# Four conditioning slots in the second layer's FFN, residual rows restored in two steps, and the first down tile staged one unit sooner

## What is computed

```python
for l in range(DEPTH):
    need_ctx = l < DEPTH - 1
    mod_x = (s_c @ w_mod[l] + b_mod[l])[:, None, :]
    mod_c = s_cc @ w_mod[l] + b_mod[l]
    ...
    h_x = _layer_norm(ALPHA * h_x + ga_x * (mix_x @ w_out[l]), ln_g[l, 0], ln_b[l, 0])
    f_x = _conv_ffn(h_x * (1.0 + cf_x) + sf_x, ffn_w_up[l], ffn_conv_w[l], ffn_conv_b[l], ffn_w_down[l])
    h_x = _layer_norm(ALPHA * h_x + gf_x * f_x, ln_g[l, 1], ln_b[l, 1])

def _conv_ffn(h, w_up, conv_w, conv_b, w_down):
    u = h @ w_up
    up = jnp.pad(u, ((0, 0), (1, 1), (0, 0)))
    u = up[:, :-2] * conv_w[0] + up[:, 1:-1] * conv_w[1] + up[:, 2:] * conv_w[2] + conv_b
    a, v = jnp.split(u, 2, axis=-1)
    return (jax.nn.silu(a) * v) @ w_down
```

## Time and profile before

| | before |
|---|---|
| median of 3 runs | 1996.57 us (1995.75 to 1996.68) |
| profiled execution | 2004.46 us |
| its span | 2002.6 us |
| mean granted TensorE clock | 0.975 |
| PE, DVE, POOL, ACT busy | 95%, 65%, 46%, 45% |
| layer 0 up stage | about 614 to 996 us of the span |
| layer 1 up stage | about 1626 to 1868 us of the span |

### The profile page before, as it was taken

The page is one execution under the profiler, slowest core; times in us unless marked ns, Lnnn a source line. Parts: engine busy times, 40 slices in busy tenths (PEclk is TensorE's granted clock), DMA queues, the critical chain, the costliest instruction groups (busy, mean ns, idle before and its releaser), DMA issues.

```text
span 2002.6 us, 32824 instructions
## 1 busy us (share of the span) xinstructions
PE 1895.2 (95%) x12510; PEld 1606.9 (80%) x12510; DVE 1307.8 (65%) x2566; ACT 898.8 (45%) x1917; POOL 926.5 (46%) x770
## 2 busy tenths in 40 slices
PE   6899799999999999999999999998999989999997
PEld 4788798867778888878888878898877778778786
DVE  3248999676585999999744263999776842222545
ACT  3224588577533222222343342565567543333442
POOL 3145467111345345553353335756432545775643
PEclk9999899999999999999999999999999999999999
DMA  8563000210111333233221121101130212222321
GB/s 349 210 241 114 26 23 22 96 49 2 43 63 43 127 126 118 93 118 117 103 74 63 53 105 64 59 28 43 43 122 1 88 47 98 105 84 91 120 98 71
DMA packets 27372, 177.31 MB, mean 89 GB/s; under 512 B 2896, under 2 KB 4048, under 8 KB 8144
## 3 DMA queue, kind: packets, MB, share of 16 engines
q1 hardware_dynamic: 22976, 158.16, 21.8%
q10 hardware_dynamic: 4240, 17.04, 2.1%
HBM read 171.00 MB, written 4.19 MB: 87 GB/s over the span
## 4 chain that ended last, share of the span: by engine, by line
PE 69%; DVE 13%; POOL 6%; issue 5%; ACT 3%; DMA 2%; SPq 0%; DVEq 0%; ACTq 0%; POOLq 0%
PE PS L1270 20%; PE PS L1165 18%; PE PS L881 9%; PE PS L875 4%; PE PS L1127 3%; PE PS L1105 3%; POOL WS L2412 3%; PE PS L1014 2%; DMA WR<-in_weights 2%; PE PS L1089 2%; DVE W L1687 2%; DVE U L1922 1%; PE PS L1095 1%; PE PS L810 1%; DVE W L2031 1%
## 5 line engine op out<-in xcount | busy, mean ns | idle before, releaser
L1270 PE MATMUL PS<-XH,WS 128*128 128x512 f32 x2016 | 543.6, 356 | 4.6 <-POOL WS L2412 4.6
L1270 PEld LDWEIGHTS PS<-XH,WS 128*128 128x128 f32 x2016 | 360.5, 190 | 60.2 <-issue 4.9
L1270 PE MATMUL PS<-XL,WS 128*128 128x512 f32 x1008 | 358.6, 356 | 0.0
L2412 POOL TENSOR_TENSOR WS<-WR,WS 128x1024 fp32r<-128x1024 f32 x88 | 215.5, 2450 | 289.1 <-ACT WS L1558 288.7
L1623 ACT ACTIVATE W<-PS,PR 128x768 f32<-128x768 f32 (+1 forms) x88 | 78.0, 886 | 424.6 <-PE PS L1270 360.7
L2241 DVE SCALAR_TENSOR_TENSOR W<-PS,PR,W 128x511 f32<-128x511 f32 (+1 forms) x132 | 83.0, 657 | 208.2 <-ACT W L1623 208.2
L1270 PEld LDWEIGHTS PS<-XL,WS 128*128 128x128 f32 x1008 | 191.5, 190 | 26.6
L881 PE MATMUL PS<-EU,XH 128*128 128x256 f32 x624 | 190.1, 305 | 5.6 <-issue 4.6
L2349 POOL TENSOR_TENSOR WL<-WR,EU 128x512 fp32r<-128x512 f32 x96 | 128.8, 1368 | 126.0 <-ACT EU L1327 126.0
L881 PE MATMUL PS<-EU,HL 128*128 128x256 f32 x624 | 182.4, 292 | 0.0
L881 PE MATMUL PS<-WL,XH 128*128 128x256 f32 x624 | 182.3, 292 | 0.0
(11 more groups left out here) (220 smaller groups left out, 4259.1 us busy)
## 6 DMA issues: line engine op xcount, KB each, us to landing
WR<-in_weights SPq DMA_DIRECT2D x128, 1024.0 KB, 4.8
U<-in_weights SPq DMA_DIRECT2D x16, 1024.0 KB, 7.5
U<-in_bias ACTq DMA_DIRECT2D x2, 1792.0 KB, 9.4
H<-in_x SPq DMA_DIRECT2D x1, 2048.0 KB, 7.8
H<-in_x ACTq DMA_DIRECT2D x1, 2048.0 KB, 14.5
U<-in_ln_rows ACTq DMA_DIRECT2D x2, 1024.0 KB, 4.8
WR<-in_weights SPq DMA_DIRECT2D x4, 512.0 KB, 3.5
kept<-H ACTq DMA_DIRECT2D x4, 512.0 KB, 2.6
```

The costliest lines, as they stand in the source:

```text
L1270: mm = pe.matmul(PS[u.pos][:, lo:hi], w[:, part, k, :], src[:, k, lo:hi], start=(k == 0 and src is xh3 and part == 0), stop=(k == KT - 1 a ...
L2412: pool.tensor_tensor(ws5[:, u.c % 2, 1], half_slot(u), ws5[:, u.c % 2, 0], ALU.subtract).then_inc(w_low, 1)
```

## The change

Three edits.

1. Slots 20 to 23 of layer 1 leave layer 0's FFN and go behind units 2, 4, 15 and 17 of layer 1's. They hold the gate of layer 1's FFN, which is read after its up stage. In layer 0 a slot stands behind units 2 to 20 without 6, 10, 14 and 18. The ring places and the counts of the semaphores follow.
2. `restore` becomes `rescale` and `shift_row`: behind the gate products of unit 5 and up, one instruction a unit, so twelve units in layer 0 (5 to 16) and eight in layer 1 (5 to 12).
3. ACT stages the first tile of the down products before the last unit's sum, in place of after it; for that the entries of the down stage are reordered so that the first tile doesn't lie in the up stage's input.

```diff
+LATE = 20
-def mods_behind(j):
+def mods_behind(l, j):
-    return int(1 < j <= 25 - EARLY)
+    if l == 0:
+        return int(1 < j <= 20 and j not in (6, 10, 14, 18))
+    return int(j in (2, 4, 15, 17))
...
-        nxt = list(range(EARLY, 24)) if l + 1 < DEPTH else []
+        nxt = list(range(EARLY, LATE) if l + 1 < DEPTH else range(LATE, 24))
...
-                   [whole(t[:, e * ENTRY:(e + 1) * ENTRY]) for t in (XH, XL, EW) for e in range(2)])
+                   [whole(t[:, e * ENTRY:(e + 1) * ENTRY]) for t, e in ((EW, 0), (XH, 0), (XH, 1), (XL, 0), (XL, 1), (EW, 1))])
...
-                u.kind, u.l, u.j, u.key = "mod", key[1] - 1, key[2], key
+                u.kind, u.l, u.j, u.key = "mod", int(key[2] >= LATE), key[2], key
...
                     if u is real[-1]:
+                        high_tiles(2 * l + 1, k_tiles[2 * l + 1][0])
                         gate(FT - 1)
                     act.wait_ge(up_sum, u.c + 1)
-                    if u is real[-1]:
-                        high_tiles(2 * l + 1, k_tiles[2 * l + 1][0])
...
-            def restore(m, t):
+            def rescale(m, t):
...
                 pool.tensor_tensor(row, row, gain, ALU.mult).then_inc(h_scaled, 1)
+
+            def shift_row(m, t):
...
                 pool.wait_ge(h_scaled, restored_by(m) + t + 1)
                 pool.tensor_tensor(row, row, offset, ALU.add).then_inc(h_ready, 1)
...
-                    if 0 <= j - 8 < restored[2 * l]:
-                        restore(2 * l, j - 8)
+                    if 0 <= j - 5 < 2 * restored[2 * l]:
+                        (rescale, shift_row)[(j - 5) % 2](2 * l, (j - 5) // 2)
```

More of the change, by code:

```diff
@@ L133, in uses @@
         u += [("out", l, n, g) for n in range(2) for g in range(KT // KDN)]
-        nxt = list(range(EARLY, 24)) if l + 1 < DEPTH else []
+        nxt = list(range(EARLY, LATE) if l + 1 < DEPTH else range(LATE, 24))
         for j in range(FT):
             u.append(("up", l, j, 0))
-            for _ in range(mods_behind(j)):
-                if nxt:
-                    u.append(("mod", l + 1, nxt.pop(0), 0))
+            for _ in range(mods_behind(l, j)):
+                u.append(("mod", 1, nxt.pop(0), 0))
         assert not nxt
@@ L740, in mods_done @@
         def mods_done(l):
-            return 24 * (l + 1) + (EARLY if has_ctx(l) else 0)
+            return 24 * (l + 1) + (EARLY if has_ctx(l) else LATE - 24)
         def half_slot(u):
@@ L1149, in spread_gates @@
                     u = [u for u in ups_of[l] if u.pos == 1][-1]
-                    wait_all(pe, (conv_done, u.done[0]), (mod_done, u.done[1]))
+                    wait_all(pe, (conv_done, u.done[0]), (mod_done, ups_of[l][-1].done[1]))
                 for hf in range(2):
@@ L2225, in ffn @@
                     if u.kind == "up" and u.half == 0:
-                        for q in mods[:mods_behind(u.j)]:
+                        for q in mods[:mods_behind(l, u.j)]:
                             mod_macs(q.key, q.mac)
-                        mods = mods[mods_behind(u.j):]
+                        mods = mods[mods_behind(l, u.j):]
                     if u.kind == "mod":
                         dve.wait_ge(mod_sum, MOD_FIRST + u.mac)
-                        mod_out(u.l + 1, u.j, PS[u.pos][:, 0:512].rearrange("p (j v c) -> p j v c", j=2, v=2))
+                        mod_out(u.key[1], u.j, PS[u.pos][:, 0:512].rearrange("p (j v c) -> p j v c", j=2, v=2))
                         continue
@@ L2386, in attention @@
                     if l > 0 and 0 <= n - 2 < restored[2 * l - 1]:
-                        restore(2 * l - 1, n - 2)
+                        rescale(2 * l - 1, n - 2)
+                        shift_row(2 * l - 1, n - 2)
                     if n in (split_at, split_at + 1):
@@ L2426, in restore @@
                     row = h3[:, t, :].rearrange("p (k c) -> p k c", c=CTX)
-                    gain, offset = lnp_mixer[:, 0:4, :], lnp_mixer[:, 4:8, :]
+                    gain = lnp_mixer[:, 0:4, :]
                 else:
-                    row = h3[:, t, :]
-                    gain, offset = lnp_of(m)[:, 0:1024], lnp_of(m)[:, 1024:2048]
+                    row, gain = h3[:, t, :], lnp_of(m)[:, 0:1024]
                 pool.tensor_tensor(row, row, gain, ALU.mult).then_inc(h_scaled, 1)
+            def shift_row(m, t):
+                if m == 1:
+                    row = h3[:, t, :].rearrange("p (k c) -> p k c", c=CTX)
+                    offset = lnp_mixer[:, 4:8, :]
+                else:
+                    row, offset = h3[:, t, :], lnp_of(m)[:, 1024:2048]
                 pool.wait_ge(h_scaled, restored_by(m) + t + 1)
```

## The result

| | before | changed |
|---|---|---|
| median of the runs, same chip | 1996.62 us (1995.75 to 2000.93, 4 runs) | 2013.34 us (4 runs, three of them 2011.95 to 2014.41) |
| ratio, 95% interval | 1 | 1.0077 [1.0057, 1.0097] |
| the same again, more runs (e7 below) | 2000.42 us (16 runs) | 2010.44 us (6 runs), 1.0054 [1.0034, 1.0073] |
| profiled execution, its span | 2004.46, 2002.6 us | 2011.95, 2010.1 us |
| mean granted TensorE clock | 0.975 | 0.976 |

The change makes the kernel slower: the ratios are 15 and 11 us. The forecast was 2004.2, the range 1992 to 2013. The sign is right. The size is at the range's edge in the first comparison (the median of 2013.34 lies just above it, the ratio on 1996.57 gives 2012) and inside it in the second. One of the four runs of the changed kernel took 4327.97 us, in a slow state; the median counts it, the ratio doesn't.

The account below looks back on a forecast made before the run. TensorE, 69% of the last chain, bounds the kernel, so time is won where it waits or runs at half clock. Terms -11 - 4.4 - 7.4 + 30.4 = +7.6 us on the 1996.57 median forecast 2004.2, range 1992 to 2013.

Parts of the forecast that it names:

- restoring in halves, layer 0: Layer 0's up stage: one POOL restoring instruction beside a slot instead of two leaves 4 of 15.1 us lost, -11 us.
- restoring in halves, layer 1: Layer 1's up stage: POOL's work in a restoring unit falls from 10.9 to 8.5 us, -4.4 us.
- first tile sooner: Both FFNs' ends: TensorE starts the down products at once, saving waits and the clock's 1.75 us each, -7.4 us.
- four slots to layer 1: Layer 1's up stage: POOL holds the slots' multiplies, TensorE stands 5.8 us a slot plus 1.75 of clock, +30.4 us.
- Rival D: FFN ends: not helped, the second tile or gate product becomes the wait; +5 us, 2009; 7%.
- The slot is ready at 16.7: Layer 1: a slot's multiplies end 16.7 us after the unit before, TensorE comes at 10.9, so waits 5.8.
- the clock costs 1.75: Layer 1: each slot's stall costs TensorE 1.75 us more through half clock, a price read from layer 0's stalls.
- Short stalls: TensorE waits cost no clock if short, read from a 1.9 us stall in layer 1 followed by 1.00.
- The port rule: VectorE and POOL: full blocking would cost 0.4 us more per POOL instruction, four slots some 4 to 6 us more.
- A: Layer 1: a slot's last two multiplies go before POOL's second low part, slots end at 14.2; -2.6 us, 1994; 15%.
- B: Layer 1: POOL doesn't hold VectorE, slots end at 9.4 and cost nothing; -22.8 us, 1973.8; 15%.
- C: Worse: slots stall 7.2 us each and layer 0 keeps 9 us, perhaps by a second late weight landing; 2015; 8%.

Follow-up runs that it names:

- e7: The changed kernel, unedited, in more runs beside the kernel before: 2010.44 us, ratio 1.0054.
- e8: Restoring in halves and first tile sooner without the four slots moved, against the kernel before, in more runs: 1977.13 us, ratio 0.9886.
- e4: Only the restoring in halves, slots and first tile staging as in the kernel before: 1984.21 us, ratio 0.9909.
- e1: Only the four slots moved to layer 1, restoring and staging as in the kernel before: 2031.07 us, ratio 1.0152.
- e3: The changed kernel with layer 1's up-weight low parts on POOL cut to 8 of 128 columns (computation incomplete): 1978.88 us, ratio 0.99.
- e9: The changed kernel with two slots in layer 1 instead of four, behind units 2 and 15: 1995.43 us, ratio 0.999 to the kernel before.
- e6: The changed kernel with layer 1's two low parts behind a slot's start made by VectorE, not POOL: 1987.76 us, ratio 0.9934 to before.

## Why the prediction was right in sign, and where its size was off

| term | forecast | by the stages of the two profiles |
|---|---|---|
| restoring in halves, layer 0 | -11 | -10.5 (366.8 - 379.0, less 1.7 of transposes) |
| restoring in halves, layer 1 | -4.4 | -4.4 (e8's 233.05 against 237.45) |
| first tile sooner | -7.4 | -7.7 (layer 0 -4.7, layer 1 -3.0) |
| four slots to layer 1 | +30.4 | +34.5 (36.2 less 1.7 of transposes) |
| sum | +7.6 | +12 |

**Restoring.** Right in mechanism and size. The remaining waits of layer 0 are six of 0.6 us rather than three of 1.3, and none cost clock.

**First tile.** Right in mechanism: the leftover in layer 1 is a wait for the convolution, as said, of 0.18 us and not 0.8. Rival D falls. The size agrees (-7.7 for -7.4), with some luck. Some 3.5 us of the forecast were the clock's 1.75 at each end, and by e4 and e1 that price is paid in the kernel before and not in others with the same wait. Also, the stretch behind layer 0's up stage (last base to layer 1's first) varies from 627.9 to 629.4 us in nine profiles with the same staging.

**Slots.** The mechanism was right down to which multiplies meet which POOL instruction. The term's size failed, in two places. "The slot is ready at 16.7": it was at 1641.33, 17.1 after the end of the unit before (1635.05 less a unit of 10.88), so the wait is 6.4 and not 5.8. And "the clock costs 1.75": 34.5 / 4 less 6.4 leaves 2.2 a slot. The 1.75 came from layer 0, where the three waits were 2.5, 2.5 and 4.8 us and the price much the same behind each. In the changed kernel the half clock lasts into TensorE's work for 3.6 and 3.8 us behind the first two slots, a price of 1.8 and 1.9 us, and for 5.0 and 4.5 behind the other two, 2.5 and 2.3; in layer 0 it lasted 3.2 to 3.4. The two together, 0.6 and 0.4 a slot, are the 4.1 us by which the term is short, and nearly all of the 4.4 that the sum lacks.

**Short stalls.** "Short stalls cost nothing extra" rested on one wait of 1.9 us. It isn't a rule of the kernel before either: its wait of 1.8 us for the first tile in layer 1 is followed by 0.50. No term of the sum fails by this.

**The port rule.** The prediction set 2.0 us for a multiply caught by a low part of 2.40 against the full length, which the Trainium skill (SBUF — State Buffer, "Who interferes with whom") would charge. In the changed kernel the pair at 1634.49 takes 5.04 where 0.90 is usual: 4.1 for two low parts of 2.40 and 2.34, 2.07 each. Single multiplies, from VectorE's timeline in slices of 0.3 us, tell why it is less than the full length:

```profile
1634.49 2.46 DVE L1688 SCALAR_TENSOR_TENSOR W<-WR,SC,W 128x256 f32<-128x256 f32 x1
1636.88 2.64 DVE L1688 SCALAR_TENSOR_TENSOR W<-WR,SC,W 128x256 f32<-128x256 f32 x1
```

The low parts run from 1634.27 to 1636.67 and from 1636.90 to 1639.24, so each multiply ends 0.28 us after the one beside it. The first was issued 0.22 us after its low part had begun and so pays only for the rest. The second, issued 0.02 us before its low part, was held all the same. The rule agrees to within 0.2 us; the surcharge of 0.4 an instruction that the prediction worked out by it was too much, since it left out where a multiply stands when the hold begins. One multiply is caught for each POOL instruction. That the slots came out 4 us dearer has the two causes above.

**Rivals.** A falls: POOL's second low part started before the last multiplies and held them. B falls by the four waits; e3, with the slots in place and hardly any hold on them, took 1978.9. C comes nearest in time, but not as described: the waits are 6.4, not 7.2, and layer 0 keeps under 4 us, not 9; TensorE has no wait for the weights after a slot, since the slot is later still.

**The level.** The forecast carried its sum over to 1996.57, and the kernel before measured 1996.62 beside the changed one, so the level held there. What was short is the difference: 7.6 against 15 by the first ratio, 11 by the second and 12 by the stages. Of these differences only the 4.4 to the stages has a cause above; that the first comparison gave more is put down to the spread of runs.

## What to carry to other kernels

An idle engine isn't a free one: VectorE was idle for most of a unit in layer 1, and sixteen multiplies of 7 us took 14.8 there, because GpSimd's instructions held them. Before work is moved to a stage with "room", list what GpSimd runs between the time it can start and the time it is due, and count one caught instruction for each. A price taken from one stall, such as the clock's, is worth reading behind several stalls first: here the same wait was followed by half clock in one kernel and by full clock in another. Where an edit bundles several changes, read each one's place alone: here two that gain 22 us hid behind one that loses 30, and the smaller repair, one instruction of GpSimd a unit instead of two, made the larger unnecessary.

## What the runs showed of the hardware that was not expected

- TensorE's clock has no fixed price per wait here. Behind waits of 6.4 us it cost 1.8 to 2.5 us in the changed kernel and 1.4 to 1.9 in e1 and e9, and the clock was at 0.50 before the wait ended. Behind 2.5 and 4.8 us in layer 0 of the kernel before it cost about 1.7. Behind the 2.3 and 1.8 us for the first tile it fell to 0.50 in the kernel before and stayed at 1.00 in e4 and e1, and behind four waits of 1.4 us in e6 it fell once. The six waits of up to 0.7 us in layer 0 had no half clock behind them.
- The same subtraction takes GpSimd 2.40 us and keeps a multiply on VectorE for 2.07 of it, and takes VectorE 1.22. So where a low part meets a slot, handing it to GpSimd makes VectorE's share of the work longer, not shorter.
- One kernel on one core, with nothing else changed, ran from 1990 to 2007 us. In the profiles of all runs the granted clock of 200 to 300 us, which no edit touches, lies between 0.86 and 0.95.
